# A two-block transformer on one core: attention of block 1 regrouped into units of two score tiles, and layer 1's modulation moved beside the feed-forward

## The chip, the core and the metric

One core of a Trainium2 chip runs the whole program. The engines are TensorE (PE; its weight loads are PEld), VectorE (DVE), ScalarE (ACT), GpSimd (POOL) and SyncE (SP), which here only issues transfers. They run their own instruction queues, each in order, and meet through semaphores. The metric is the device time of one execution in microseconds (us); smaller is better.

## What is computed

Two blocks of two layers each, in float32, batch 1, 512 latent tokens, 1024 features. Block 1 (layers 0 and 1) also carries 256 context tokens; its layer 1 no longer updates them.

```python
m_lat = split(silu(c) @ w_ada[li] + b_ada[li], 6)       # and m_ctx: the modulation, 6 x 1024 numbers a layer
h = rms_norm(x, g_mix) * (1 + m_lat[1]) + m_lat[0]
p = h @ w_in[li]                                        # 9 groups of 256 columns
y = concat([fourier_mix(p[:G]),
            diff_attention(p[G:4G]),                    # 4 heads, two softmaxes each, 32 wide:
                                                        #   (a0 - lam * a1) @ v, then rms_norm over 64 (the sub-norm)
            na_attention(p[4G:7G]),                     # 4 heads, 64 wide, one softmax, window bias for latent keys
            chunk_gmlp(p[7G:])])
x = x + m_lat[2] * (y @ w_out)
x = x + m_lat[5] * conv_ffn(rms_norm(x, g_ffn) * (1 + m_lat[4]) + m_lat[3])
```

Latent queries see 768 keys (512 latent and 256 context), context queries the 256 context keys. Context queries exist only in layer 0. The modulation depends on `c` and `c_ctx` alone; layer 1's is needed first by layer 1's first norm. Block 2 is another pair of layers and is not touched.

## The kernel before, in words

**Stages.** Every engine has one program (lines 2560 to 2660), the same stages in the same order: start, then for each layer of block 1 norm, projection, attention, output projection and feed-forward. There is no planner; the order on each engine is that in which the Python emits it.

**Attention of block 1** (`att_units`, line 648). The unit of work is one head for one query tile of 128: 48 units in layer 0 (2 head pairs x 6 query tiles x differential and neighbourhood x 2 heads), 32 in layer 1. `pipeline` (line 279) emits the units: in iteration u it first advances the older ones in flight, oldest first, then starts unit u, then one piece of work "beside". Each unit has four segments:

- *TensorE* (`tensor_attend`, 702): scores, with full 128-row queries that POOL has masked to the head's rows (`QM`, made at 978), against 128-row keys (721); a differential unit makes two score tiles one after the other, a neighbourhood unit one. Two iterations later up to six transposes (733), one later the value products (742) into 64 rows of bank 6.
- *VectorE* (`vector_attend`, 795): bias (838, neighbourhood and latent only), maximum (808), negated scale (810), reciprocal of the sum (815); for differential units also -lambda/sum (828), scaling of the first tile (829) and the combination with the second (831). Later the copy of 512 transposed columns (852).
- *ScalarE* (`scalar_attend`, 899): exponentials with sum (914, 922, 925), scaling for neighbourhood units (928), copy of the other 256 transposed columns (935), copy of the result into `Y` (939).
- *POOL* (`gpsimd_attend`, 966): the masked queries.

The relative-position table `TB` is loaded when the projection has read `HL` (690) and VectorE adds the window to it (800), ahead of everything else in its attention.

**Work beside** (`beside_items`, 663): statistics of the gated MLP's norm ("stat": POOL squares at 991, VectorE sums at 859, ScalarE logarithm and exponential at 945 and 947, VectorE product at 866), gated MLP, Fourier mixing, and in layer 0 the modulation: 8 pairs for layer 0 itself and 12 pairs for layer 1. A modulation pair is two 1 MB weight loads, 32 matmul records on four 32-column tiles (360), a copy by ScalarE (368), eight small records that sum and turn (374), and one VectorE instruction (381). All share bank 7, one after the other. Layer 0 gets one item an iteration, layer 1 one every third.

**After the units**: the sub-norm of `Y` columns 2 and 3 (ScalarE square 959, TensorE 790 and 792, ScalarE logarithm and exponential 962 and 964 with an activation table load each, VectorE 896).

**Output projection** (`tensor_out`, 1132; splits at 1144 to 1185). Weights are split into a high and a low part (ScalarE 1074, VectorE 1081 or POOL 1088), three views ahead; ScalarE makes three such casts before its first cast of `Y` (1153). The split of every `Y` column waits for all of attention (`y_made`, 1117). SP loads the weights as jobs of two views into three ring slots (`sync_feed`, 1041); a slot is free when both views of its former job are split.

**Feed-forward of layer 0** (`tensor_ffn` 1345, `scalar_ffn` 1375, `vector_ffn` 1405): 22 "up" steps of two views each, eight records of 768 columns times three parts a view, with four groups of eight "down" views among them. `beside` there is advanced once a step and used only in layer 1 and 2 for rotary tables.

## Time and profile before

| | |
|---|---|
| median of 3 runs | 4641.05 us (4635.44 to 4645.61) |
| the profiled execution | 4640.21 us, its span 4638.4 us |
| TensorE busy | 4199.6 us, 91% of the span |
| VectorE, ScalarE, POOL busy | 1810.7, 1468.8, 1106.0 us |
| granted TensorE clock, mean | 0.946 |

How to read it: times in the trace count from the span's start. A busy TensorE is modelled from pipelined matmuls, so the start-to-start distance of two blocks is the better measure of a rate. A float32 matmul stands as two records, a transpose as one. PEclk is the granted TensorE clock as a share of 2.4 GHz. "x8" merges eight instructions into one row. What stands in brackets is the engine's idle time before the row and what ended it.

### The profile page before, as it was taken

To read this page: it belongs to the slowest core of one execution; us is meant where nothing else is said; L and a number is where in the kernel's file an instruction comes from. 1 tells how busy PE (TensorE), PEld (TensorE's weight loads), DVE (VectorE), ACT (ScalarE), POOL (GpSimd) and SP (SyncE) were. 2 spreads that over 40 slices of the span, in tenths; PEclk is the share of its full clock that TensorE was granted. 3 is DMA by queue.
4 is the path that set the end of the run, shared out by engine and by line. 5 is a ranking of instruction groups with operands and counts; after the bars stand their busy time and mean duration, and the time that the engine had idled before them with its cause. 6 is when DMAs were issued, how large, how long until landed. Compare 5 with 4: busy or idle time off the path is not lost.

```text
span 4638.4 us, 57661 instructions
## 1 busy us (share of the span) xinstructions
PE 4199.6 (91%) x24256; PEld 3065.1 (66%) x24256; DVE 1810.7 (39%) x3078; ACT 1468.8 (32%) x2290; POOL 1106.0 (24%) x713
## 2 busy tenths in 40 slices
PE   7979889999897979999888889899998887898998
PEld 4756568888665558874445567688744455676886
DVE  1146433333214633433855421234338544213333
ACT  3245423222334433330242222333312322233332
POOL 1000132222200033331010134433210110354332
PEclk9989889999998989999998889999999988999999
DMA  4014511111101012212100022222211000222221
GB/s 187 19 61 160 222 46 55 66 64 60 66 28 47 19 63 95 96 64 73 59 19 15 25 73 95 76 91 96 89 38 59 24 10 25 74 96 71 100 96 59
DMA packets 56592, 322.35 MB, mean 69 GB/s; under 512 B 5648, under 2 KB 5776, under 8 KB 27920
## 3 DMA queue, kind: packets, MB, share of 16 engines
q1 hardware_dynamic: 56336, 318.67, 19.4%
q8 instruction: 193, 3.16, 0.3%
q14 instruction: 63, 0.52, 0.0%
HBM read 316.55 MB, written 2.10 MB: 69 GB/s over the span
## 4 chain that ended last, share of the span: by engine, by line
PE 78%; DVE 11%; ACT 5%; issue 3%; POOL 2%; DMA 1%; SPq 0%; POOLq 0%; DVEq 0%; ACTq 0%
PE ps L1101 47%; PE ps L1563 5%; PE ps L547 4%; PE ps L538 3%; PE ps L2005 3%; PE ps L721 2%; PE ps L742 2%; PE ps L322 1%; PE ps L360 1%; PE ps L733 1%; PE ps L2085 1%; POOL WL L1088 1%; DVE ar L1819 1%; DVE small L1815 1%; PE ps L781 1%
## 5 line engine op out<-in xcount | busy, mean ns | idle before, releaser
L1088 POOL TENSOR_TENSOR WL<-ring,WH 128x1024 fp32r<-128x1024 f32 (+4 forms) x262 | 572.3, 2185 | 1153.8 <-ACT WH L1074 1132.0
L1074 ACT ACTIVATE WH<-ring 128x1024 fp32r<-128x1024 f32 (+4 forms) x408 | 397.7, 977 | 1293.0 <-PE ps L1101 1287.2
L1101 PE MATMUL ps<-FH,WH 128*128 128x512 f32 x1760 | 602.6, 375 | 42.7 <-POOL FL L1271 37.7
L1101 PE MATMUL ps<-FH,WL 128*128 128x512 f32 x1760 | 599.5, 374 | 0.0
L1101 PE MATMUL ps<-FL,WH 128*128 128x512 f32 x1760 | 595.1, 371 | 0.0
L1436 DVE SCALAR_TENSOR_TENSOR ftmp<-ps,vec,ftmp 128x511 f32<-128x511 f32 (+2 forms) x440 | 302.0, 695 | 347.6 <-ACT ftmp L1393 193.1
L1081 DVE TENSOR_TENSOR WL<-ring,WH 128x1024 fp32r<-128x1024 f32 (+4 forms) x146 | 164.1, 1129 | 639.0 <-ACT WH L1074 638.9
L1101 PEld LDWEIGHTS ps<-FH,WH 128*128 128x128 f32 x1760 | 309.0, 190 | 114.2 <-issue 45.2
L1101 PEld LDWEIGHTS ps<-FL,WH 128*128 128x128 f32 x1760 | 310.4, 190 | 60.2
L1101 PEld LDWEIGHTS ps<-FH,WL 128*128 128x128 f32 x1760 | 308.6, 190 | 59.9
L1101 PE MATMUL ps<-AH,WH 128*128 128x512 f32 x880 | 308.2, 383 | 9.8 <-DVE AL L1441 9.8
L1101 PE MATMUL ps<-AH,WL 128*128 128x512 f32 x880 | 299.9, 374 | 0.0
L1101 PE MATMUL ps<-AL,WH 128*128 128x512 f32 x880 | 297.9, 371 | 0.0
L1563 PE MATMUL ps<-HL,ring 128*128 128x512 f32 x448 | 199.7, 602 | 4.3 <-DVE HL L1555 3.6
L721 PE MATMUL ps<-ar,HC 128*128 128x256 f32 (+1 forms) x432 | 156.7, 498 | 33.6 <-ACT ar L914 31.2
L1101 PEld LDWEIGHTS ps<-AH,WH 128*128 128x128 f32 x880 | 155.0, 190 | 44.4 <-DVE AL L1441 11.4
L1459 POOL TENSOR_TENSOR ftmp<-ftmp 128x512 f32<-128x512 f32 (+1 forms) x88 | 126.1, 1433 | 219.6 <-DVE ftmp L1436 219.2
L1101 PEld LDWEIGHTS ps<-AL,WH 128*128 128x128 f32 x880 | 155.0, 190 | 34.2 <-issue 4.3
L1101 PE MATMUL ps<-GH,WH 128*128 128x512 f32 x384 | 153.2, 399 | 23.7 <-POOL GL L2528 23.7
L1101 PEld LDWEIGHTS ps<-AH,WL 128*128 128x128 f32 x880 | 154.2, 189 | 29.5
L1563 PEld LDWEIGHTS ps<-HL,ring 128*128 128x128 f32 x448 | 86.2, 194 | 112.6 <-issue 108.1
L978 POOL TENSOR_TENSOR HC<-ar,cst 128x512 f32<-128x512 f32 (+1 forms) x40 | 32.9, 844 | 527.1 <-PE ps L721 334.0
(404 smaller groups left out, 7261.9 us busy)
## 6 DMA issues: line engine op xcount, KB each, us to landing
ring<-in_wup SPq DMA_DIRECT2D x88, 1024.0 KB, 4.8
ring<-in_wada SPq DMA_DIRECT2D x30, 1024.0 KB, 6.4
ring<-in_wgate SPq DMA_DIRECT2D x24, 1024.0 KB, 4.8
ring<-in_wdown SPq DMA_DIRECT2D x24, 896.0 KB, 4.7
ringb<-in_wada SPq DMA_DIRECT2D x18, 1024.0 KB, 6.4
ring<-in_wout SPq DMA_DIRECT2D x16, 1024.0 KB, 4.8
ring<-in_wdown SPq DMA_DIRECT2D x12, 1024.0 KB, 5.0
ring<-in_wbr SPq DMA_DIRECT2D x24, 512.0 KB, 3.3
```

The lines of the kernel that those rows point to most:

```text
L538: mm = e.matmul(pr[:, b * 512:b * 512 + 256], h[:, k, :], wt[:, k * 256:k * 256 + 256], start=k == 0, stop=k == 7)
L547: mm = e.matmul(pr[:, c:c + n], wt[:, k * 256 + j * 128:k * 256 + j * 128 + 128], h[:, k, :], start=k == 0, stop=k == 7)
L721: mm = e.matmul(pr[:, n:n + b - a], q, PF[:, base + jt, a:b], start=True, stop=True)
L742: mm = e.matmul(bank(6)[p0:p0 + 64, 0:128], PT[:, b, col + h * 64:col + h * 64 + 64], tmp1(3)[:, x * 128:x * 128 + 128], start=x == 0, sto ...
L1074: e.activation(wh, view, ACT.Copy).then_inc(*whi_a.up(L, n))
L1081: e.tensor_tensor(wl, view, wh.bitcast(F32), SUB).then_inc(*wlo_v.up(L, n))
L1088: e.tensor_tensor(wl, view, wh.bitcast(F32), SUB).then_inc(*wlo_g.up(L, n))
L1101: mm = e.matmul(out[:, c:c + h.shape[1]], ww[:, k, :], h, start=at == 0 and p == 0, stop=at == K - 1 and p == 2)
L1436: e.scalar_tensor_tensor(out=dst, in0=src, scalar=conv_cols(L, ch, a), in1=dst, op0=MUL, op1=ADD).then_inc(*(ffn_v.up(L, "tap", x, j, c) i ...
L1459: e.tensor_tensor(zg, zg, zv, MUL).then_inc(*ffn_g.up(L, x))
L1563: mm = e.matmul(out, wt[:, k * step + off:k * step + off + 128], HL[:, k, :], start=k == 0, stop=k == 7)
L2005: mm = e.matmul(out, wt[:, k * step + off:k * step + off + 128], HL[:, k, :], start=k == 0, stop=k == 7)
```

## The change

1. `att_units` now lists units of two score tiles: a differential unit is one head (its two softmaxes), a neighbourhood unit is a head pair. 36 units in layer 0, 24 in layer 1, in the order: two differential units of query tile g, then the neighbourhood unit of g-1.
2. Scores are made without masked queries: the two tiles use the head's own 32 (differential) or 64 (neighbourhood) rows of queries and keys, issued in turn into two different bank pairs. `QM` and POOL's masking go. A unit's scores wait until the unit before has been read.
3. Transposes go to banks 4 (copied by VectorE) and 5 (copied by ScalarE), three blocks each; the weights of two heads lie in two buffers in the space that `QM` had, and the value products of two heads are issued in turn into the two halves of bank 6. ScalarE copies 128 rows at once.
4. The scaling of a differential unit's first tile moves from VectorE (829) to ScalarE. The two reciprocals become one of two columns.
5. The window is added to `TB` by POOL, as its first instruction in attention.
6. The sub-norm runs as work beside, column by column and (layer 0) in a 512- and a 256-part, in a new buffer `adab`. The order in which `Y` is split and used becomes 0, 1, 6, 7, 2, 4, 3, 5.
7. Layer 1's 12 modulation pairs move to layer 0's feed-forward: one part or sum before each "up" view. Their weights go to `adab`, one part at a time; the transfers are issued by SP in between those of the weight jobs, and the first of them right behind job 0.
8. Beside items are placed by a plan: layer 0 one an iteration, layer 1 one every second.

The core of the diff (the engines' programs in attention are shown where the order of instructions matters):

```diff
+        E = [[tmp1(0), tmp1(1)], [tmp1(2), tmp1(3)]]
+        WT = [hcf[:, 768 * i:768 * i + 768] for i in range(2)]
...
+            groups = [(jt, *q) for jt in range(2) for q in qts]
+            for g in range(len(groups) + 1):
+                if g < len(groups):
+                    out += [(groups[g][0], "diff", hh, *groups[g][1:]) for hh in range(2)]
+                if g:
+                    out.append((groups[g - 1][0], "na", None, *groups[g - 1][1:]))
...
+            for x, it in enumerate(beside_items(l)):
+                plan[x if l == 0 else 2 * x].append(it)
+            for j in (2, 3):
+                for p in range(2 if l == 0 else 1):
+                    plan[last_diff(l, j) + 4 + p].append(("sq", j, p))
+                    plan[last_diff(l, j) + 5 + p].insert(0, ("root", j, p))
...
@@ tensor_attend, unit
+                if u:
+                    w.wait_ge(*scores_taken(l, u - 1, 0), *scores_taken(l, u - 1, 1))
+                for c, d_ in kcols:
+                    for a in range(2):
+                        r = slice(64 * hh + 32 * a, 64 * hh + 32 * a + 32) if sort == "diff" else slice(64 * a, 64 * a + 64)
+                        mm = e.matmul(two(a)[:, n:n + d_ - c], PF[r, BASE[kq] + jt, qc:qc + 128], PF[r, BASE[kk] + jt, c:d_],
+                                      start=True, stop=True)
...
+                for x, b in enumerate(vb):
+                    for a in range(2):
+                        mm = e.matmul(bank(6)[64 * a:64 * a + 64, 0:128], PT[:, b, c:c + 64], WT[a][:, x * 128:x * 128 + 128], start=x == 0,
+                                      stop=x == len(vb) - 1)
...
@@ vector_attend, unit: segment 1 bias, maximum, shift of both tiles; then
+                w.wait_ge(soft_a.at(l, u, "exp", 0), soft_a.at(l, u, "exp", 1))
+                e.reciprocal(inv, total).then_inc(*soft_v.up(l, u, "inv"))
+                if sort == "diff":
+                    e.tensor_scalar(top[:, 0:1], inv[:, 1:2], nlam, None, MUL).then_inc(*soft_v.up(l, u, "nlam"))
+                    w.wait_ge(soft_v.at(l, u, "nlam"), soft_a.at(l, u, "w0"))
+                    e.scalar_tensor_tensor(out=E[u % 2][0][:, 0:n], in0=E[u % 2][1][:, 0:n], scalar=top[:, 0:1], in1=E[u % 2][0][:, 0:n],
+                                           op0=MUL, op1=ADD).then_inc(*soft_v.up(l, u, "w"))
...
@@ scalar_attend, unit: segment 1 exponentials of both tiles; then
+                w.wait_ge(soft_v.at(l, u, "inv"))
+                for a in range(1 if sort == "diff" else 2):
+                    e.activation(x, x, ACT.Copy, scale=inv[:, a:a + 1]).then_inc(...)
...
@@ gpsimd_attend
+            w.wait_ge((in_rpb, 16 * (l + 1)))
+            e.tensor_tensor(TB2, TB2, C("win")..., ADD).then_inc(*tb_g.up(l))
...
+        def mods1_after(j):
+            out = [] if j else [0]
+            for i in range(1, 24):
+                t = MODS1.index(("part", i - 1))
+                if (view_of(0, "up", t // 2, t % 2) + 7) // 2 == j:
+                    out.append(i)
+            return out
@@ sync_feed, after the load of job j
+                for i in mods1_after(j) if L == 0 else ():
+                    w.wait_ge(*([mod_mm.at(1, i - 1, "part")] if i else [sub_v.at(0, 2, 1), sub_v.at(0, 3, 1)]))
+                    for r in range(2):
+                        e.dma_start(adab[:, r, :], d["wada"][1, i][:, 1024 * r:1024 * r + 1024]).then_inc(ada_in[r], 16)
...
+        MODS1 = [(x, i + b) for i in range(0, 24, 2) for x, b in (("part", 0), ("part", 1), ("sum", 0))]
...
@@ tensor_ffn
+                        next(beside, None)
@@ scalar_ffn, vector_ffn
-                next(beside, None)
                 for j in range(2):
+                    if L == 0 or j == 0:
+                        next(beside, None)
```

## Rows read from the trace of the kernel before

**Rows 1.** Busy time by stretch: us, each engine with its instructions, granted clock, DMA share, GB/s

```profile
400.00:530.00 130.00, 127.84 (x1123) 89.94 (x1123) 81.45 (x215) 67.32 (x163) 8.06 (x10) 1.00 0.64 243
530.00:562.00 32.00, 19.69 (x136) 11.26 (x135) 5.06 (x9) 15.10 (x17) 0.00 (x0) 0.62 0.54 220
1465.00:1625.00 160.00, 144.98 (x766) 99.23 (x766) 108.71 (x220) 77.55 (x173) 8.57 (x10) 0.96 0.06 20
720.00:760.00 40.00, 40.00 (x232) 35.02 (x231) 16.00 (x24) 11.65 (x13) 10.92 (x5) 1.00 0.20 67
2650.00:2670.00 20.00, 11.28 (x196) 7.05 (x187) 6.63 (x14) 4.51 (x5) 0.00 (x0) 0.60 0.00 1
```

**Rows 2.** Timeline of layer 1's attention, TensorE: start, us, instructions

```profile
1530.92 0.87 PE L733 MATMUL ps<-cst,ar 128*128 128x128 f32 x6
...
1531.63 2.75 PE L721 MATMUL ps<-ar,HC 128*128 128x512 f32 x8
```

**Rows 3.** Timeline of layer 1's attention, VectorE and ScalarE

```profile
1449.80 0.68 DVE L838 SCALAR_TENSOR_TENSOR ar<-ps,HL 128x512 f32<-128x512 f32 x1
...
1452.75 0.16 DVE L815 RECIPROCAL small<-small 128x1 f32<-128x1 f32 x1 [1.10 <-ACT ar L922]
...
1452.95 0.94 ACT L928 ACTIVATE ar<-ar,small 128x768 f32<-128x768 f32 x1 [0.23 <-DVE small L815]
...
1453.79 0.25 ACT L939 ACTIVATE ar<-ps 64x128 f32<-64x128 f32 x1
...
1453.94 0.36 ACT L935 ACTIVATE ar<-ps 128x256 f32<-128x256 f32 x1
...
1465.28 0.95 DVE L808 TENSOR_REDUCE small<-ps 128x1 f32<-128x768 f32 x1
...
1468.52 0.16 DVE L815 RECIPROCAL small<-small 128x1 f32<-128x1 f32 x1 [0.89 <-ACT ar L914]
...
1469.50 1.02 DVE L831 SCALAR_TENSOR_TENSOR ar<-ar,small 128x768 f32<-128x768 f32 x1
```

**Rows 4.** Timeline where layer 1's attention starts

```profile
1422.84 2.32 POOL L991 TENSOR_TENSOR ar<-ar 128x256 f32<-128x256 f32 x4
...
1428.83 4.16 DVE L800 TENSOR_TENSOR HL<-HL,cst 128x3840 f32<-128x3840 f32 x1 [44.23 <-DMA HL<-in_rpb]
...
1438.06 0.41 DVE L859 TENSOR_REDUCE small<-ar 128x4 f32<-128x256 f32 x1
...
1443.69 0.43 DVE L866 TENSOR_TENSOR ar<-ar,small 128x256 f32<-128x256 f32 x1 [2.70 <-ACT small L947]
```

**Rows 5.** Timeline of layer 0's attention, TensorE, with a modulation pair

```profile
459.51 1.93 PE L360 MATMUL ps<-ring,silp 128*32 128x256 f32 x32
...
461.37 1.52 PE L742 MATMUL ps<-ar 128*64 128x128 f32 x12
...
464.83 0.95 PE L374 MATMUL ps<-cst,modp 128*128 128x2 f32 x8
...
465.71 1.52 PE L742 MATMUL ps<-ar 128*64 128x128 f32 x12
```

**Rows 6.** Timeline of block 2's recurrence, TensorE: two row tiles

```profile
2411.06 0.69 PE L2011 MATMUL ps<-cst,ring 64*128 64x512 f32 x1
...
2411.06 0.69 PE L2013 MATMUL ps<-cst,ring 64*128 64x512 f32 x1
```

**Rows 7.** Timeline, ScalarE, where the two attention stages end

```profile
558.67 2.94 ACT L1074 ACTIVATE WH<-ring 128x1024 fp32r<-128x1024 f32 x3
...
1631.15 1.28 ACT L962 ACT_TABLE_LOAD   x1
...
1634.44 0.63 ACT L964 ACTIVATE ar<-ar 128x512 f32<-128x512 f32 x1
```

**Rows 8.** DMA issues of layer 0's feed-forward: count, KB each, median us to landing

```profile
ring<-in_wup SPq DMA_DIRECT2D x18, 1024.0 KB, 4.8
```

More of the change, by code:

```diff
@@ L668, in beside_items @@
             if l == 0:
-                out += [(x, li, i) for li, a in ((0, 8), (1, 0)) for i in range(a, 24, 2) for x in ("parts", "sum")]
+                out += [(x, 0, i) for i in range(8, 24, 2) for x in ("parts", "sum")]
             return out
@@ L795, in vector_attend @@
         def vector_attend(e, w, l):
[L796 removed]
+            units = att_units(l)
             nlam = tiny[:, 85:86]
[L798 to L804 removed]
@@ L856, in item @@
+            def item(it):
                 if it[0] == "stat":
@@ L929, in unit @@
-                yield 1
-                yield 1
-                if kind == "lat":
-                    w.wait_ge(turn_mm.at(l, u))
-                    if u:
-                        w.wait_ge(pv_mm.at(l, u - 1))
-                    e.activation(tmp1(3)[:, 512:n], two(2)[:, 512:n], ACT.Copy).then_inc(*wt_a.up(l, u))
+                top, shift, total, inv = soft_stat(u)
+                biased = sort == "na" and kind == "lat"
+                if u >= 2:
+                    w.wait_ge(*(turn_mm.at(l, u - 2, c, k) for c, _, k in turns_of(l, u - 2)))
@@ new lines, in unit @@
+                for a in range(2) if biased else ():
+                    w.wait_ge(qk_mm.at(l, u, a))
+                    e.activation(E[u % 2][a][:, 512:n], two(a)[:, 512:n], ACT.Copy, scale=0.125).then_inc(*soft_a.up(l, u, "ctx", a))
+                for a in range(2):
+                    x = E[u % 2][a][:, 0:n]
+                    w.wait_ge(soft_v.at(l, u, "shift", a))
+                    if biased:
+                        w.wait_ge(soft_a.at(l, u, "ctx", a))
+                    e.activation(x, x if biased else two(a)[:, 0:n], ACT.Exp, bias=shift[:, a:a + 1],
+                                 scale=1.0 if biased else 32 ** -0.5 if sort == "diff" else 0.125,
+                                 accum_out=total[:, a:a + 1]).then_inc(*soft_a.up(l, u, "exp", a))
@@ L991, in item @@
                         e.tensor_tensor(LB[:, 256 * (t % 4):256 * (t % 4) + 256], v, v, MUL).then_inc(*loc_g.up(l, t))
-            pipeline([unit(u, *x) for u, x in enumerate(units)], beside(l, item))
+            pipeline([unit() for _ in att_units(l)], beside(l, item))
         def chunks_of(n):
@@ L1132, in tensor_out @@
         def tensor_out(e, w, l):
-            last, turns = len(att_units(l)) - 1, soft_turns(l)
+            last = len(att_units(l)) - 1
             segs = segs_of(l)
```

361 lines of the change are left out of this document (178 added, 183 removed).

## The prediction

> **What bounds the kernel now.** I read the busy time by stretch first, because the average over the span hides the stages. The change touches four stretches: the attention of layer 0 (about 257 to 562 us), the attention of layer 1 (1421 to 1643), and, since work moves there, the feed-forward of layer 0 (678 to 1190); the rest of the span is untouched. In attention TensorE is busy 127.8 of 130 us in layer 0 and 145.0 of 160 in layer 1, VectorE 81 and 109, ScalarE 67 and 78 [rows 1]. So TensorE sets the pace there. Layer 1 has eight groups of four units in those 160 us: 20.0 us a group. Only the end of layer 0's stretch is slack: after the last unit, from about 530, modulation pairs run alone, with the clock granted at 0.62 [rows 1]. In the feed-forward TensorE is busy 40.00 of 40 us [rows 1]: whatever is put on it there costs its full price.
>
> The timeline of one unit says what TensorE pays: two score tiles 2.75 us for eight records (2.57 us of steady streaming), six transposes 0.87 (0.65 start to start), six value products 1.52 [rows 2, 5]. A group of two differential and two neighbourhood units is 2 x 5.1 + 2 x 3.9 = 18.0 us of TensorE out of 20.
>
> **What the edits do to TensorE.** Scores: each unit now issues two tiles on different row tiles into different banks. Block 2 has such a pair: two 64-row, 512-column matmuls start at the same 2411.06 us [rows 6]. Halving takes 3 x 1.28 = 3.8 us off a group. Values: pairs in column tiles; the modulation's four 32-column tiles run 32 records of 256 columns in 1.86 us [rows 5], about 58 ns each, where one alone would be some 213, so a pair should fit in the time of one: another 3 us. TensorE then needs 18.0 - 3.8 - 3 = some 11 us a group. It no longer sets the pace, and the question is what comes next.
>
> The Trainium skill (TensorEngine Tiling, Key Properties) says that changing the tiling mode, not just the tile, drains TensorE, and the new units change it three times each. That rule speaks against the row and column tiles; it gives no figure. In the trace the four-tile block is followed by two-tile work 1.86 us after its start and shows no gap beyond its own 1.93 us [rows 5]. I put 0.1 us on each insertion in the feed-forward and nothing on it in attention, where TensorE has slack; at 0.5 us a change attention would still not move, and the feed-forward would take 15 more.
>
> **What is late next: a chain through ScalarE and VectorE.** VectorE's queue in iteration u is: copies of unit u-2, combine of u-1, maxima of u. ScalarE's: value copy of u-3, weights copies of u-2, scaling of u-1, exponentials of u. The scaling waits for the exponentials of u-1, the combine waits for the scaling, the maxima stand behind the combine, the exponentials behind the maxima: one serial loop. Steps from rows:
> - maxima of both tiles to both exponentials done: 1468.52 - 1465.28 = 3.2 us [rows 3];
> - scaling 0.94, combine 1.02 (0.94 to the next start) [rows 3];
> - ScalarE's copies ahead of the scaling: value copy 0.15 start to start, weights copy of 384 columns about 0.38 (256 columns take 0.36) [rows 3];
> - a biased tile, bias to sum: 1452.75 - 1449.80 = 2.95, and the second tile adds 0.68 + 0.95 + 0.15 = 1.8.
>
> Second differential unit: 0.15 + 2 x 0.38 + 0.94 + 0.94 + 3.2 = 6.0. Neighbourhood unit behind it: 0.15 + 0.38 + 0.94 + 0.03 + 0.94 + 2.95 + 1.8 = 7.2. First differential unit behind that has no combine ahead: 0.38 + 2 x 0.83 + 2 x 1.05 = 4.2 on ScalarE. Group: **17.4 us** against 20.0. The three removals on VectorE (the first tile's scaling, a third of each weights copy, one reciprocal) are in these numbers; the scaling has only moved to ScalarE, where it is on the loop.
>
> **Starts.** The bias add leaves VectorE (4.16 us, and the wait for its table before it) for POOL, so the first maxima come some 8 us sooner. But POOL's squares now queue behind it, and VectorE waits for them in its first beside item. Before, that item began at 1438.06. Now: table at 1428.8, the add on POOL (3840 columns; 256 take 0.58, so at most 8.7 and, with the fixed part off, I take 8), squares 0.6: 1437.5. The start gains 0.5 us a layer, nothing more; were POOL as quick as VectorE it would be 4. The statistics keep their 6 us an item, 1438.06 to 1444.1 [rows 4].
>
> **Layer 1.** Statistics and three units to 1466; then 8 x 7.2 + 6 x 6.0 + 6 x 4.2 = 119 us; beside copies 2; the first sub-norm, now in the loop on ScalarE (3.9 us with its two table loads, 1631.15 to 1635.07, plus a square) 4.4 [rows 7]; TensorE queueing behind Fourier items and some cold stretches 12, an estimate. That is 1603.5 for the last exponential; two more scalings, copies, transposes and value products of the last unit 6.5; the second sub-norm 3.9: 1614, against 1635.1: **-21 us**.
>
> **Layer 0.** Statistics (three items) and three units to 303, as before. Then one more unit, 5.5; eight latent groups less the first units, 8 x 7.2 + 6 x 4.2 + 6 x 6.0 = 119; four context groups at 256 columns, 8.2 each, 33; TensorE queueing 12; ScalarE's beside items (4 Fourier copies, 8 modulation copies, 0.5 each) and VectorE's overhang 7; the first column's sub-norm in two parts 8.3: 488 for the last exponential, 491 for the last value copy, and, after two parts with two table loads each (7.7), 499 for the last sub-norm. Before, this point was 558.7, where the weight casts start [rows 7]: -60. Of these, some 50 are the twelve modulation pairs that leave, the last of which ran alone.
> Then a **new wait**: the first modulation load for layer 1 is queued on SP behind weight job 0 and waits for the last sub-norm, since it lands in the buffer that the sub-norm uses. Jobs 1 and 2 stand behind it. ScalarE's third weight cast needs job 1 and stands ahead of the casts of Y. A 1 MB load lands in 4.8 us [rows 8]; behind another MB I take 7.6 (about 2.8 us a MB, an estimate: 243 GB/s at a DMA share of 0.64 [rows 1] makes 380 GB/s in full), so job 1 arrives some 8.5 us after the sub-norm, where the cast would have been due 2 us after: +7. Net of layer 0's attention: **-53 us**.
>
> **Feed-forward of layer 0.** Twelve pairs, each 1.86 for the parts and 0.88 for the sum [rows 5]: 32.9 us, all on the path. 36 insertions at 0.1 us: 3.6. Loads: one buffer, so the load of part i waits for part i-1. In six pairs out of twelve the odd part comes one view (8.3 us, 48 of 232 records in 40) later while a ring job is ahead of it in the queue: landing near 10.7 us against a need at 9.25, 1.5 x 6 = 9. What ScalarE and VectorE do for a pair lies beside: they are busy 11.7 and 16.0 of 40 us there [rows 1]. **+45 us**; bounds 33 (no gap, no stall) and 60 (each odd part 2 us late).
>
> **Sum.** -53 - 21 + 45 = -29 us. The profiled execution took 4640.2, its span 4638.4, and the median of the runs is 4641.05, 0.8 above; so 4612 on the median's scale. A measurement of this kernel tells a change from none at about 0.2%, 9.3 us.
>
> **Rivals.**
 Cold, a group needs some 21 us of TensorE and it is the bound again: 3.7 x 8 = 30, less the 9 already taken, +21: 4632, the same as before within the measurement. Against it: layer 0 has modulation beside, and a cold engine is a busier one. Chance 0.17. The Trainium skill (TensorE: Matmul & The Clock Gate, Loop structure matters more than you think) says that matmuls stay warm or not by the loop nest, and that waits between them make them run cold. By that rule this rival would come true; the row of 0.60 agrees.
> - *The modulation starves the feed-forward* (slower). Place: the odd part's wait for its load. A load that waits behind two others, at 2.8 us for each MB more, is 10 us under way. If each of the twelve odd parts waits 5 us, that is 60, not 9, and the time 4662; it turns the sign at 3.3 us a part. For it: a single buffer. Against it: DMA is only 20% busy there [rows 1]. Together with a loop 10% longer than I count: 0.14.
> - *The loop is shorter*: copies overlap, table loads fall into ScalarE's waits, job 1 is in time. 10% of 290 us of loop and the 7: about 4578. Chance 0.19.
> - *Row tiles don't overlap* in fp32: TensorE 15 of 17.4 us and the scores at 2.8 us, about when the combine ends: 4620. It lies within the forecast.
>
> **How the numbers follow.** Forecast (4595 to 4628) 0.50, shorter 0.19, clock 0.17, slower 0.14. Faster takes the first two and a part of the third, 0.74; same 0.13; slower 0.13. Range 4578 to 4650: from the short loop to just past no change.
>
> **What would show it.** Groups in layer 1 near 17.4 us with VectorE or ScalarE ending most waits; TensorE about 65% busy there; first maxima near 1424 but first statistics still near 1437 less the shift; a gap of some 7 us on ScalarE ahead of its third weight cast of layer 0; the feed-forward of layer 0 longer by 36 to 60. Wrong if attention keeps TensorE above 85%, if a group is over 19 us, or if the feed-forward grows by more than 60.

## The result, and the profile after

The changed kernel takes 4668.5 us (median of 7 runs, 4657.6 to 4673.9), the kernel before 4638.8 in the same session: a ratio of 1.0058, with a 95% interval of 1.0045 to 1.0072. By the ratio it is **slower by some 27 us** (the medians are 29.7 us apart), where 29 us less were forecast. The profiled execution took 4657.6 us with a span of 4655.8.

Three marks divide the span for everything below: TensorE's first sum of squares in layer 0's output projection (P0, which stands a tile and a half behind that projection's start, so that waits at its start are in it), its first scores of layer 1 (S1), and its first sum of squares in layer 1's output projection (P1). In the changed kernel they are these lines of TensorE's timeline (start, us, instructions, the idle time before them):

```profile
567.99 1.24 PE L324 MATMUL ps<-ytmp,cst 128*128 128x512 f32 x3
...
1457.12 1.56 PE L773 MATMUL ps<-ar 32*128 32x512 f32 x8 [0.78 <-ACT ar L608]
...
1680.59 1.02 PE L324 MATMUL ps<-ytmp,cst 128*128 128x512 f32 x2
```

| stage | before | after | difference | forecast |
|---|---|---|---|---|
| to P0 (all up to the start of layer 0's output projection; the changed part is its attention) | 586.7 | 568.0 | -18.7 | -53 |
| P0 to S1 (output projection and feed-forward of layer 0, norm and projection of layer 1) | 835.7 | 889.1 | +53.4 | +45 |
| S1 to P1 (layer 1's attention, start of its output projection) | 233.0 | 223.5 | -9.5 | -21 |
| sum | 1655.3 | 1680.6 | +25.3 | -29 |

Behind P1 nothing is changed; in the profiled executions of all kernels here that rest takes between 2974 and 2989 us, so spans of single executions are not compared below, but the stages. Each mark comes from one execution: P0 to S1, all but the same in this kernel and in eight of the runs below (e1, e5, e6, e9, e13, e14, e16, e17), lies between 887.5 and 892.2 us there, so a difference of 2 or 3 us in it says nothing.

Busy time by stretch of the kernel after (columns as in [rows 1]: us, PE, PEld, DVE, ACT, POOL with their instructions, granted clock, DMA share, GB/s):

```profile
303.00:400.00 97.00, 83.03 (x523) 52.02 (x520) 63.95 (x145) 55.84 (x123) 0.00 (x0) 0.89 0.13 44
400.00:505.00 105.00, 79.21 (x657) 51.69 (x658) 53.27 (x126) 62.78 (x130) 0.00 (x0) 0.80 0.32 121
505.00:560.00 55.00, 29.79 (x173) 19.58 (x174) 22.14 (x38) 23.13 (x45) 13.01 (x6) 0.69 0.20 77
720.00:760.00 40.00, 39.16 (x264) 31.63 (x252) 12.62 (x20) 13.11 (x16) 11.62 (x6) 1.00 0.34 118
1484.00:1650.00 166.00, 120.70 (x786) 74.98 (x787) 100.07 (x201) 102.06 (x197) 0.00 (x0) 0.84 0.04 14
```

TensorE is no longer full in attention: 162 of 202 us in layer 0 and 121 of 166 in layer 1, where [rows 1] had 128 of 130 and 145 of 160. No engine is; each waits for another, and the granted clock in layer 1 has gone from 0.96 to 0.84. In the feed-forward it is 39.2 of 40 us busy, as before.

The sub-norm's place in layer 1, TensorE's and ScalarE's timeline:

```profile
1569.40 0.61 ACT L985 ACTIVATE adab<-ar 128x512 f32<-128x512 f32 x1
1570.16 2.05 PE L817 MATMUL ps<-adab,cst 128*128 128x512 f32 x2 [6.26 <-ACT adab L985]
1572.00 1.38 PE L784 MATMUL ps<-cst,ar 128*128 128x128 f32 x6
1573.31 1.56 PE L773 MATMUL ps<-ar 32*128 32x512 f32 x8
...
1578.14 1.28 ACT L989 ACT_TABLE_LOAD   x1
1579.44 0.69 ACT L989 ACTIVATE adab<-ps,cst 128x512 f32<-128x512 f32 x1
1580.14 1.28 ACT L991 ACT_TABLE_LOAD   x1
1580.18 5.27 PE L842 MATMUL ps<-ring,ar 128*128 128x512 f32 x8 [5.31 <-ACT adab L989]
...
1585.38 1.53 PE L798 MATMUL ps<-HC,ar 128*64 128x128 f32 x24
```

Here is what the forecast did not have. The sum of squares (L817) stands in TensorE's queue ahead of the next unit's transposes and scores, and the square that it waits for stands on ScalarE behind both exponentials: TensorE stands still for 6.3 us. One iteration later the Fourier product (L842) wants PSUM bank 7, which the logarithm reads; that stands behind two more exponentials and a table load: another 5.3 us, and then the product runs cold, 5.3 us where it takes 3.7 at full clock. Values, transposes and scores are behind it.

The end of layer 0's attention, ScalarE and SP's queue:

```profile
533.12 1.99 ACT L1114 ACTIVATE WH<-ring 128x1024 fp32r<-128x1024 f32 x2
533.82 0.80 SPq L1089 DMA_DIRECT2D adab<-in_wada  x2
534.67 2.37 SPq L261 DMA_DIRECT2D ring<-in_wout  x3
542.21 1.06 ACT L1114 ACTIVATE WH<-ring 128x1024 fp32r<-128x1024 f32 x1 [7.11 <-DMA ring<-in_wout]
```

The third cast waits 7.1 us for a job that is queued behind the first modulation load: as forecast, 7.

The start of layer 1's attention, VectorE and POOL:

```profile
1458.68 0.96 DVE L871 TENSOR_REDUCE small<-ps 128x1 f32<-128x768 f32 x1 [38.93 <-PE ps L773]
...
1464.01 8.27 POOL L1004 TENSOR_TENSOR HL<-HL,cst 128x3840 f32<-128x3840 f32 x1 [93.33 <-DMA HL<-in_rpb]
1472.23 2.33 POOL L1018 TENSOR_TENSOR ar<-ar 128x256 f32<-128x256 f32 x4
1472.88 0.42 DVE L896 TENSOR_REDUCE small<-ar 128x4 f32<-128x256 f32 x1 [12.00 <-POOL ar L1018]
```

The order is as forecast: the first maxima come 1.6 us after the first scores. The first statistics come 15.8 us after the scores, against 15.7 in the kernel before, so the 0.5 us that the forecast took for a start is not there.

The groups of TensorE's instructions between 680 and 1280 us that are the modulation (parts, sums; busy us, mean ns, idle time before them; eleven of the twelve pairs, the first begins at 640.6 us, ahead of that window), and the places where its load is on the chain of work that ended last (start, us):

```profile
L1405 PE MATMUL ps<-adab,silp 128*32 128x256 f32 x352 | 25.2, 392 | 8.6 <-DMA adab<-in_wada 8.6
...
L376 PE MATMUL ps<-cst,modp 128*128 128x2 f32 x88 | 10.4, 241 | 0.0
```

```profile
692.04 7.71 DMA adab<-in_wada
752.98 6.46 DMA adab<-in_wada
...
1089.19 6.12 DMA adab<-in_wada
```

There are six such places, one for every second pair, as counted beforehand. TensorE waits for these loads 8.6 us in all, 1.9 us at most at a time; the forecast had 9.

### The profile page after: what moved, and what is told of

It is laid out like the page before. It is cut to its first block, busy times and chain, and to the rows that moved or that the text cites. A ratio compares the mean times of both kernels' runs of the same rounds, so it can differ in the third digit from the quotient of the medians.

```text
span 4655.8 us, 57676 instructions
## 1 busy us (share of the span) xinstructions
PE 4136.1 (89%) x24256; PEld 2999.5 (64%) x24256; DVE 1760.1 (38%) x2974; ACT 1496.2 (32%) x2304; POOL 1089.6 (23%) x675
## 4 chain that ended last, share of the span: by engine, by line
PE 70%; DVE 11%; issue 8%; ACT 6%; POOL 3%; DMA 2%; SPq 0%; POOLq 0%; DVEq 0%; ACTq 0%
PE ps L1141 46%; PE ps L1637 5%; PE ps L2079 3%; PE ps L549 2%; PE ps L324 1%; DVE small L871 1%; POOL WL L1128 1%; DMA adab<-in_wada 1%; PE ps L798 1%; PE ps L540 1%; PE ps L773 1%; PE ps L2159 1%; PE ps L784 1%; DVE ar L1893 1%; DVE small L1889 1%
## 5 line engine op out<-in xcount | busy, mean ns | idle before, releaser
L1141 PE MATMUL ps<-GH,WL 128*128 128x512 f32 x384 | 152.0, 396 | 0.0
L1141 PE MATMUL ps<-GL,WH 128*128 128x512 f32 x384 | 150.8, 393 | 0.0
```

The costliest lines, as they stand in the source:

```text
L1141: mm = e.matmul(out[:, c:c + h.shape[1]], ww[:, k, :], h, start=at == 0 and p == 0, stop=at == K - 1 and p == 2)
```

## The experiments

Two theories at first. **Queue**: the sub-norm beside the units, priced in the forecast at its time on ScalarE, holds TensorE's queue and bank 7, and costs two to three times that. **Clock**: attention falls short since TensorE, now with pauses, runs at the lower level. All ratios are against the kernel before, with their 95% intervals. The marks of the profiled executions:

| run | to P0 | P0 to S1 | S1 to P1 | ratio |
|---|---|---|---|---|
| kernel before | 586.7 | 835.7 | 233.0 | 1 |
| changed kernel | 568.0 | 889.1 | 223.5 | 1.0058 |
| e1_subnorm_end | 549.6 | 887.5 | 217.0 | 1.0002 |
| e5_sum_one_later | 553.8 | 892.2 | 218.1 | 1.0032 |
| e4_warm | 587.1 | 883.7 | 240.2 | 1.0127 |
| e9_squares_first | 565.0 | 887.7 | 216.9 | 1.0053 |
| e2_no_mods | 560.8 | 844.4 | 224.2 | 0.9933 |
| e3_one_load | 566.0 | 878.7 | 223.4 | 1.0028 |
| e6_first_load_later | 561.1 | 890.6 | 226.1 | 1.0050 |
| e7_mods_in_attention | 615.7 | 844.3 | 223.8 | 1.0056 |
| e10_copy_later | 620.0 | 841.9 | 217.0 | 1.0045 |
| e8_best | 608.7 | 840.9 | 206.3 | 0.9991 |
| e11_before_wider | 583.3 | 835.8 | 235.3 | 1.0002 |
| e13_best_mods_ffn | 537.5 | 891.6 | 204.6 | 0.9934 |
| e14_copy_same | 530.4 | 889.9 | 206.3 | 0.9916 |
| e16_roots_shared | 526.5 | 889.8 | 203.0 | 0.9907 |
| e17_both | 525.9 | 889.3 | 203.9 | 0.9908 |

### e1_subnorm_end: the sub-norm undone

```
 beside_plan:
-            for j in (2, 3):
-                for p in range(2 if l == 0 else 1):
-                    plan[last_diff(l, j) + 4 + p].append(("sq", j, p))
-                    plan[last_diff(l, j) + 5 + p].insert(0, ("root", j, p))
 tensor_attend, after the pipeline (scalar_attend and vector_attend likewise, as before the change):
+            for j in (2, 3):
+                w.wait_ge(sub_a.at(l, j, 1 - l, "sq"), *scores_taken(l, last, 0), *scores_taken(l, last, 1))
+                mm = e.matmul(two(j - 2)[:, 0:512], C("b64"), tmp1(j)[:, 0:512], start=True, stop=True)
```

> The changed kernel with one part undone: the sub-norm of both columns after the last unit, in the two score tiles, as before the change. Changed kernel: ratio 1.0058 to the kernel before, about 4668 us. Theory 'the sub-norm beside holds up TensorE's queue': in layer 1 it costs about 14 us where it stands (the iteration of 32.4 us for a group that takes 18.4), in layer 0 about 15; at the end a column costs 4 to 5 us more in each layer. So shorter by 18 to 22 us: about 4648, ratio 1.0015. Rival 'it costs no more than its time on ScalarE' (4.4 and 8.3 us, which are paid at the end too): no change within 4 us, 4668. Rival 'the clock explains the short gain of attention': no change either, with the granted clock still 0.83 to 0.85 in the loops.

Measured: 4638.5 us, 1.0002 [0.9994, 1.0011], 26 us less than the changed kernel. Expected were 18 to 22. Its marks have 18.4 us of it in layer 0 (2.0 of them ahead of the first scores, where nothing was edited) and 6.5 in layer 1. The cost stands: the sub-norm beside was dearer than the sub-norm at the end, by 25 us, in a change that put it there to be hidden. The group of units that took 32.4 us in layer 1 takes 22.7; in layer 0 one that took 35.1 takes 15.4.

The loops by themselves, from the first scores of a layer to its last, are 257.8 us (layer 0) and 179.3 (layer 1) in the changed kernel, 240.3 and 169.3 in e1. So the first column's sub-norm costs the loops 17.5 and 10.0 us; the forecast had 8.3 and 4.4. What follows the last scores is 1.2 and 3.5 us longer in e1.

The groups of e1 in layer 1 say something besides, with no sub-norm among them: from one neighbourhood unit's scores to the next they take 18.3, 22.7, 17.7, 22.7, 17.7 and 18.8 us. The two of 22.7 are those in which a Fourier product stands beside the group's first differential unit. The second of them in e1's timeline (TensorE and VectorE):

```profile
1549.67 5.56 PE L838 MATMUL ps<-ring,ar 128*128 128x512 f32 x8
...
1555.16 1.53 PE L794 MATMUL ps<-HC,ar 128*64 128x128 f32 x24
...
1557.21 0.56 DVE L892 COPY HC<-ps 128x384 f32<-128x384 f32 x1 [5.26 <-PE ps L780]
```

Values and transposes of older units are behind the product in TensorE's queue; VectorE's copy of the transposed weights waits 5.3 us for them, and the combination and the next maxima stand behind that copy. The product runs cold here (5.6 us, 5.0 in the other group, 3.7 at full clock), which is at most 1.9 of the 5.0 us. So TensorE's queue is a part of the loop even where an item waits for nothing.

### e5_sum_one_later: the same place on ScalarE, another on TensorE

```
-                    plan[last_diff(l, j) + 5 + p].insert(0, ("root", j, p))
+                    plan[last_diff(l, j) + 5 + p].insert(0, ("root", j, p))
+                    plan[last_diff(l, j) + 5 + p].insert(0, ("sqm", j, p))
+                    plan[last_diff(l, j) + 6 + p].insert(0, ("prod", j, p))
 and the other items, which use bank 7 too, are placed around the iterations of "sqm"
```

> The changed kernel with the sub-norm still beside the units, but its TensorE sum one iteration after the square, no other user of the eighth PSUM bank in that iteration, and the product on VectorE one more iteration later. ScalarE's own work (square, two table loads, two activations) is the same and in the same place. Theory 'queue': most of the excess goes, 10 us in layer 1 and 8 in layer 0 (the second column's tail stays): about 4650. Rival 'the table loads on ScalarE are the price': within 3 us of the changed kernel, 4668.

Measured: 4651.3, 1.0032 [1.0019, 1.0045]: 12 us less than the changed kernel by the ratios, 17 by the medians; its marks say 14.2 in layer 0 and 5.4 in layer 1, of which its feed-forward, 3 us longer in that execution, hides a part. So between half and four fifths of e1's gain is there, although ScalarE does the same work at the same place. The sum no longer waits (TensorE's timeline of this run, with ScalarE's square ahead of it):

```profile
1558.94 0.61 ACT L994 ACTIVATE adab<-ar 128x512 f32<-128x512 f32 x1
...
1559.87 2.08 PE L826 MATMUL ps<-adab,cst 128*128 128x512 f32 x2
...
1569.84 3.70 PE L851 MATMUL ps<-ring,ar 128*128 128x512 f32 x8
```

The loops are 246.9 and 175.4 us, 6.6 and 6.1 more than in e1: 12.7 us, which is what the forecast had for this work (8.3 and 4.4). What lies above the forecast, another 14.8 us in the changed kernel, is therefore no time of ScalarE's but comes from where the sum stands. The edit changes two things together, the place of the sum in TensorE's queue and the neighbours in bank 7; what each is worth was not separated.

### e4_warm: more work for TensorE while it waits

```
+                for _ in range(4):
+                    e.matmul(bank(bk)[:, 0:256], C("ident"), C("cos1")[:, 0:256], start=True, stop=True)
                 for a, blocks, bk in turns_of(l, u):
                     w.wait_ge(soft_v.at(l, u, "w") if sort == "diff" else soft_a.at(l, u, "w", a))
```

> The changed kernel with four extra 256-column products of a constant in every unit of both attentions, issued while TensorE waits for the weights to transpose and written over by the transposes; results unchanged. They take 0.85 us at full clock. Rival 'clock': the granted clock rises from 0.84 to over 0.95 in the loops, Fourier blocks fall from 5.3 to 3.7 us and modulation parts from 3.6 to 1.9, and the time falls by 15 to 25 us, to about 4648. Theory 'queue, and the serial loop through VectorE and ScalarE': those blocks mostly lie beside, the gain is under 8 us, and where the extra work delays a transpose it is lost again: 4660 to 4672.

Measured: 4695.6, 1.0127 [1.0114, 1.0140], 32 us **more** than the changed kernel. Neither theory said so. The granted clock did rise (0.92 against 0.88 in 1500 to 1650), and the Fourier product came down to 3.7 us, but four extra products took 1.9 us and not 0.85 (an fp32 product is two records; by the 3072 columns in 2.57 us of [rows 2] eight records of 256 columns are 1.7 us), and the transposes behind them start late:

```profile
1560.60 3.70 PE L846 MATMUL ps<-ringb,ar 128*128 128x512 f32 x8
1564.14 1.89 PE L783 MATMUL ps<-cst 128*128 128x256 f32 x8
1565.87 0.82 PE L788 MATMUL ps<-cst,ar 128*128 128x128 f32 x6
1566.62 1.56 PE L773 MATMUL ps<-ar 32*128 32x512 f32 x8
```

I had sized the extra work wrongly, so the run does not give the price of the clock. It shows something else: 60 units with 1.9 us more each, 114 us, cost 32, although TensorE had pauses of 27% on average. Its pauses are not where its work is. A higher clock without that work was not tried.

### e9_squares_first: the order on POOL

```
+            for t in range(4):
+                squares(t)
             TB2 = TB.rearrange("p h y x -> p (h y) x")
             w.wait_ge((in_rpb, 16 * (l + 1)))
             e.tensor_tensor(TB2, TB2, C("win")...
```

> The changed kernel with POOL's squares of the first four row blocks issued before its 8.3 us add of the window to the bias table, instead of behind it. Theory 'the add on POOL is what keeps the first statistics late': the first statistics sum on VectorE comes 8 us sooner in each layer, the table is ready 2.5 us later than now, still before the third unit: shorter by 10 to 16 us, about 4655. Rival 'the third unit then waits for the table': shorter by less than 5 us.

Measured: 4659.9, ratio 1.0053 [1.0041, 1.0065]; its interval overlaps the changed kernel's. The gain is 2 us by the ratios and 9 by the medians; the marks show 3.0 us in layer 0 and 6.6 in layer 1. All are less than the 10 to 16 expected. The statistics do start at once, but their product on VectorE stands still while POOL adds (VectorE's and POOL's timeline of this run):

```profile
1459.49 8.26 POOL L1013 TENSOR_TENSOR HL<-HL,cst 128x3840 f32<-128x3840 f32 x1 [5.70 <-DMA HL<-in_rpb]
...
1460.62 7.75 DVE L903 TENSOR_TENSOR ar<-ar,small 128x256 f32<-128x256 f32 x2 [3.13 <-ACT small L981]
```

Two products that take 0.43 us each elsewhere end at 1468.4, 0.6 us after POOL is done. The Trainium skill (SBUF — State Buffer, Who interferes with whom) says that a VectorE instruction which holds the SBUF ports that it shares with GpSimd, and one of GpSimd, exclude each other for their whole length; its section on the two sides of SBUF counts two SBUF inputs on VectorE among the cases. The trace agrees: 7.75 us for two products of two SBUF inputs. ScalarE, TensorE's transposes and the next maxima wait behind these products, not for the table, so the rival's reason did not come true, and whether its size did the ratios and the medians leave open.

### e2_no_mods and e3_one_load: what the feed-forward's 53.4 us are

e2 leaves out layer 1's modulation and uses layer 0's in its place; e3 leaves out the weights of all parts but the first.

```
e2: -        MODS1 = [(x, i + b) for i in range(0, 24, 2) for x, b in (("part", 0), ("part", 1), ("sum", 0))]
    +        MODS1 = []
    -                for i in mods1_after(j) if L == 0 else ():
    +                for i in ():
e3: -                for i in mods1_after(j) if L == 0 else ():
    +                for i in [0] if L == 0 and j == 0 else ():
    -                    w.wait_ge((ada_in[r], 16 * (i + 1)))
    +                    w.wait_ge((ada_in[r], 16))
```

> The changed kernel without layer 1's modulation: neither its loads nor its products nor its sums are there, and layer 1 uses layer 0's modulation instead. Changed kernel: ratio 1.0058, about 4668. Theory 'the whole growth of layer 0's feed-forward, 54 us by the two traces, is the twelve modulation pairs, and the 7 us wait of the third weight cast is their first load': shorter by 58 to 62 us, about 4608, ratio 0.993. Rival 'part of the growth is something else in the feed-forward': shorter by less than 50. Beside the kernel before, which has these pairs under its attention, it would say what the regrouped attention, sub-norm as it is, gives when TensorE has no layer-1 modulation anywhere.

> The changed kernel with all 24 modulation parts of layer 1 taken from one load, so that no part waits for its weights and 23 MB are not loaded; the products are all there. It leaves out the weights of parts 1 to 23 (layer 1's modulation is computed from the first part's). Theory 'the price in the feed-forward is TensorE's own time, 36 us and more, the waits for loads are about 9 to 14': shorter by 9 to 14, about 4656. Rival 'starved feed-forward': shorter by over 25, below 4643.

Measured: e2 4608.7, 0.9933 [0.9917, 0.9950]; e3 4652.5, 1.0028 [1.0017, 1.0040]. Both times are as expected. The marks split the 53.4, each term to within the 2 or 3 us of one execution: reloads 889.1 - 878.7 = **10.4** us (forecast 9), products and insertions 878.7 - 844.4 = **34.3** (forecast 36.5), together 44.7 against 45 in the forecast. But e2, with no modulation there at all, still takes 844.4 where the kernel before takes 835.7: **8.7 us** that are no part of the modulation (e7, e10 and e8, also without it there, take 844.3, 841.9 and 840.9). This is e2's rival, and for its size the marks decide, not the time. It comes in very small pieces. Busy time by stretch of the kernel before, and of e2:

```profile
800.00:1000.00 200.00, 200.00 (x1148) 175.15 (x1147) 62.47 (x96) 47.66 (x53) 52.19 (x26) 1.00 0.21 69
```

```profile
800.00:1000.00 200.00, 200.00 (x1134) 174.27 (x1133) 62.74 (x96) 48.99 (x54) 50.38 (x24) 1.00 0.19 64
```

Both are full and at the full clock, and yet 1148 records go through in one and 1134 in the other: 1.2% slower, with nothing to wait for.

### e11_before_wider: is it where the tiles lie?

```
 modp = sb("modp", [P, 2, 512])
+adab = sb("adab", [P, 2, 1024])
```

> The kernel before with nothing but the 8 KB tile added that the change allocates; no instruction uses it, but all tiles behind it lie 8 KB further in every partition. In the two changed kernels that have no modulation in layer 0's feed-forward, TensorE's pairs of 512 and 256 columns follow each other every 0.353 us there, in the kernel before every 0.349, and the stage from the first output projection to layer 1's first scores takes 866 us against 857. Theory 'the placement of the tiles does that': slower by 8.7 us, ratio 1.0019. Rival 'it comes with the program, not with the tiles': ratio 1.0000.

Measured: 4642.2, 1.0002 [0.9994, 1.0011], and 835.8 us from P0 to S1. A shift of the tiles by 8 KB is not it. e8 below, without that tile, has 1134 records again. The rate goes with the program, in a way that no run here explains.

### e6_first_load_later

```
-            out = [] if j else [0]
+            out = [0] if j == 2 else []
```

> The changed kernel with the first modulation load behind weight job 2 instead of job 0 on SP, so that jobs 1 and 2 do not wait for the last sub-norm. Theory 'that wait costs 7 us': 4661, and the gap of 7.1 us on ScalarE before its third weight cast is gone. Rival 'the output projection would wait for the casts of the values anyway': under 2 us.

Measured: 4664.6, 1.0050 [1.0032, 1.0068]: by the ratios not to be told from the changed kernel. In the profile the gap is gone and P0 comes 6.9 us sooner; the two stages behind it were 4 us longer together in that execution. The place is confirmed by the mark, the gain of the whole only within its interval.

### e7, e10: the modulation back beside the attention

```
e7:  -                plan[x if l == 0 else 2 * x].append(it)
     +                plan[(x if x < 19 else 19 + (x - 18) // 2) if l == 0 else 2 * x].append(it)
e10: sub-norm at the end as in e1, and on ScalarE
     -                    scalar_mod(e, w, it[1], it[2], bank(7))
     +                    pending.append(it[1:])
     and flush() of what is pending ahead of the next unit's exponentials
```

> The changed kernel with layer 1's modulation back beside layer 0's attention, as before the change, but with the sum of one pair and the parts of the next in the same iteration, so that the 20 pairs of both layers fit in 21 iterations. Theory 'TensorE has room there and none in the feed-forward': the feed-forward falls by 54 us, the 7 us wait goes, layer 0's attention grows by some 2 us a pair, 24 us: shorter by 37, about 4631, ratio 0.998. Rival 'each pair holds up the queue or its 2 MB come too late': attention grows by 45 or more, 4652, ratio 1.003.

> The kernel with the sub-norm at the end (ratio 1.0002, 4639 us) with layer 1's modulation back beside layer 0's attention, one pair in one iteration, and ScalarE's copy of a pair's parts one iteration later, ahead of the exponentials instead of behind them, in which ScalarE had waited 48 us for the parts of 20 pairs. Theory 'the pairs cost what ScalarE waits for them, TensorE has the room': the feed-forward gives 45 us back, the wait of the third cast 7, layer 0's attention grows by 15: 4602, ratio 0.992. Rival 'the parts hold up TensorE's queue all the same, since they wait for VectorE's sum (28 us over 19 pairs)': attention grows by 35 or more: 4622, ratio 0.9965.

Measured: e7 4664.3, 1.0056 [1.0037, 1.0075]; e10 4662.3, 1.0045 [1.0033, 1.0057]. Both rivals, and worse. The feed-forward gives back 45, and layer 0's attention takes it all: P0 comes 47.7 us later in e7 than in the changed kernel, and 70.3 later in e10 than in e1, although no 7 us wait is left. For each of twelve pairs, with the gap of 7 us that went, that makes 4.6 us in e7 and 6.5 in e10; a pair cost 3.7 in the feed-forward. One iteration of e10, in order of time:

```profile
447.00 1.05 PE L376 MATMUL ps<-cst,modp 128*128 128x2 f32 x8 [0.40 <-ACT modp L370]
...
449.61 0.16 DVE L383 TENSOR_TENSOR small<-ps,vec 128x8 f32<-128x8 f32 x1
...
449.82 3.64 PE L362 MATMUL ps<-ring,silp 128*32 128x256 f32 x32 [1.77 <-DVE small L383]
453.39 2.31 PE L794 MATMUL ps<-HC,ar 128*64 128x128 f32 x24
...
455.75 0.28 ACT L987 ACTIVATE ar<-ps 128x128 f32<-128x128 f32 x1 [5.03 <-PE ps L794]
```

TensorE waits for VectorE's sum, then the parts run cold (3.64 us against 1.93 in [rows 5]), then come the values, and ScalarE waits 5.0 us for them with the scaling behind. In the kernel before, TensorE was the bound, busy 127.8 of 130 us at a granted clock of 1.00, and a pair took 2.7 us of its time there [rows 5]. In the regrouped attention a pair is neither hidden nor cheap. Which of the two places is better is less clear: e7 has the ratio of the changed kernel (1.0056 and 1.0058). e10 is 20 us slower than e1, but it also has the later copy, which e14 below finds to cost 7.1 us for eight pairs; by that rate its twenty pairs would have 18 us of it (an estimate).

### e8, e13, e14, e16, e17: towards a kernel that beats both

```
e13 (on e1): first modulation load without its wait for the sub-norm; scalar_mod one iteration later, as e10;
     squares(t) for t in range(4) ahead of all on POOL; in vector_attend, first statistics item, before the products:
+                    if 0 in it[1]:
+                        w.wait_ge((in_rpb, 16 * (l + 1)))
+                        e.tensor_tensor(TB2, TB2, C("win")..., ADD).then_inc(*soft_v.up(l, "tb"))
     sub-norm at the end: Ln, Ln, Exp, Exp in place of Ln, Exp, Ln, Exp
e8:  e13 with the modulation beside the attention (as e10), and no adab
e14: e13 with scalar_mod in the same iteration
e16: e13 with a statistics item's Ln, Ln, Exp, Exp
e17: both
```

> As the run above, and besides: POOL's first four squares ahead of everything, the window added to the bias table by VectorE while ScalarE takes the first roots (4.2 us on VectorE, in a wait of 6), the two columns' logarithms together and their exponentials together at the end (two table loads less a layer), and the 8 KB tile of the modulation's loads not allocated. Theory: 10 us sooner at each of the two starts, 2.6 at each end, and 8.7 in the feed-forward if the placement of the tiles is what makes its products 1.4% slower: 4602 - 20 - 5 - 9 = 4568, ratio 0.985. Rival 'the starts are given back, since the third unit waits for its table and the loop for the weights' transposes': 4590.

> The kernel with the sub-norm at the end (4639 us) and layer 1's modulation left in the feed-forward, its first load not waiting for the sub-norm; besides, as in the second run of these four: squares first, the table by VectorE, the copy of the parts one iteration later, tables loaded once for both columns. Theory: 7 for the wait of the third cast, 20 for the two starts, 5 for the ends: 4607, ratio 0.993; the difference to the second run, 39 us, is what the place of the modulation and the tile cost. Rival 'starts given back': 4625.

> The fastest kernel so far (sub-norm at the end, modulation in the feed-forward, squares first, table by VectorE; ratio 0.9934, 4609 us) with ScalarE's copy of layer 0's modulation parts back behind the exponentials of the same iteration. Theory 'that copy waits for cold parts and holds up the loop': longer by 8 us (8 pairs, 1 us each): 4617, ratio 0.995. Rival 'it changes nothing, since with the later copy the sum waits in TensorE's queue instead': 4609.

> The fastest kernel so far (4609 us) with the two logarithms of a statistics item together and then the two exponentials, so that an item has two table loads (1.28 us each) instead of four. Theory 'ScalarE's table loads lie on the serial loop': five items, 2.6 us each less, 13 us, but in the first item of each layer VectorE's table add of 4.2 us now ends last, so 10: 4599, ratio 0.991. Rival 'ScalarE's time beside is hidden': under 3 us.

> The run with ratio 0.9934 with both edits: the copy of the parts in the same iteration (0.9916 alone) and one pair of table loads a statistics item (0.9907 alone). Theory 'different places, they add up': 0.9934 - 0.0018 - 0.0027 = 0.989, about 4590. Rival 'they share a wait, or each was a matter of the placement of the program': 0.9907, 4598.

Measured: e8 4632.5, 0.9991 [0.9981, 1.0002], far from 4568: it carries e10's price, the later copy of twenty pairs included. e13 4609.2, 0.9934 [0.9922, 0.9946], as expected. Layer 1's attention is down to 204.6 us from 217.0 in e1, 12.4 for the start and the tables. VectorE's add lies in ScalarE's root time, out of POOL's way.

e14: 4602.5, 0.9916 [0.9903, 0.9930], where slower or the same was expected. Its interval overlaps e13's a little, but the marks agree that it is faster. With the later copy TensorE's sums wait 11.9 us for it in 303 to 505 us, with the copy in place 2.8; P0 comes 7.1 sooner. The later copy, of e10 too, was a mistake of mine: it took a wait off ScalarE and put it on TensorE's queue. TensorE's groups of e13 and of e14 in that stretch:

```profile
L376 PE MATMUL ps<-cst,modp 128*128 128x2 f32 x64 | 10.2, 282 | 11.9 <-ACT modp L370 11.9
```

```profile
L376 PE MATMUL ps<-cst,modp 128*128 128x2 f32 x64 | 9.5, 271 | 2.8 <-ACT modp L370 2.8
```

e16: 4598.1, 0.9907 [0.9893, 0.9920], as expected: P0 comes 11.0 us sooner than in e13, layer 1's attention is 1.6 shorter. So the table loads of the statistics lie on the loop, more in layer 0 (three items) than in layer 1 (two; in the first the exponentials are done at 1424.9 and the products begin at 1427.2, when VectorE's table add ends). e17: 4595.6, 0.9908 [0.9894, 0.9921]: its rival; the two do not add up (P0 at 525.9 against 526.5). The fastest kernels here are e16 and e17 (e14 is within their intervals), **0.9% faster than the kernel before**, 1.5% than the changed one.

## Why the prediction was wrong

Forecast 4612, measured 4668.5, outside the range of 4578 to 4650 and of the other sign.

- **The step that failed: "one serial loop" of ScalarE and VectorE alone, with what stands beside it priced at its own time and TensorE's queue put at 12 us a layer ("TensorE has slack").** The runs show TensorE's queue inside that loop: whatever holds it delays the transposes, and through VectorE's copies the next maxima. By the marks the forecast missed by 54 us: 34 in layer 0's attention, 12 in layer 1's, 8 in the feed-forward.
- **Its clearest term: "the first sub-norm, now in the loop on ScalarE 4.4" and, in layer 0, "the first column's sub-norm in two parts 8.3".** 12.7 us, measured 27.5 (17.5 and 10.0). The item was followed neither through TensorE's queue nor through bank 7. It makes a group 32.4 us long that takes 22.7 in e1, and in layer 0 35.1 instead of 15.4. e5, without touching ScalarE's work, brings it back to 12.7. With this term alone right the forecast would have been 4627, still 12 us below the kernel before: out of the loops it takes the slowdown away (e1 is at 1.0002), but it is not all of the miss.
- **Its larger term: layer 0's loop without the sub-norm, some 20 us.** The forecast has the last exponential at 488, 479.7 without its 8.3; in e1 it is done at 499.6. The forecast gave TensorE's queue 12 and the other items 7 there. Groups of a latent neighbourhood unit and two latent differential units, forecast at 17.4, take 20.5 to 21.4 in e1's layer 0, with an item in every iteration, and 17.7 in its layer 1 where no Fourier product stands beside the first differential unit. Four of the eight parts run cold in e1's layer 0, 1.7 us more each, and two Fourier products of 256 columns, 1 us more each, so the clock can be 9 of these 20 (an estimate). Which item costs how much was not separated: that TensorE's queue is the cause here is read from timelines, and no run shows it by itself.
- **Layer 1's loop.** "17.4 us a group" was 18.3, 21.6, 19.2, 17.7 and 19.0 where no sub-norm is. The last exponential is done 187.7 us after S1 where the forecast has 181.1, and 5.6 of these 6.6 us are the sub-norm; so its 12 for TensorE's queue was about right here. From there to the last value copy it takes 11.6 us and not 6.5: the last unit was priced too low.
- **The modulation in the feed-forward, +45**: 44.7 by e2 and e3, both terms within 2.2 us. The rival "the modulation starves the feed-forward" found its place, six reloads on the chain, but not its size: 8.6 us of waits in all, near the 9 that were counted, not 60.
- **8.7 us that no step had**: TensorE's products of layer 0 run 1.2% slower at full clock in every kernel with the new attention and no modulation in the feed-forward. Not a shift of the tiles (e11). Open.
- **Row tiles and column tiles**: eight records of two score tiles take 1.56 us against 2.75 [rows 2], 24 value records 1.53 against 1.52 for 12. They do what the forecast says. "TensorE has slack in attention" was true on average (80% busy in layer 0, 73% in layer 1) and false for what it was used for: that extra work in the queue costs nothing.
- **The 7 us at the third cast** were right, the starts nearly so (nothing in place of 0.5 us); that a later load can take the 7 us away is shown by its gap in e6, not by e6's time.
- **The rival of the clock**: granted 0.84 in place of 0.96, and cold parts and Fourier products. Half of the rival came true: the clock fell. But its group of 21 us, with TensorE as the bound, did not: TensorE is 73% busy in layer 1. And e1 and e5 changed the time while the clock stayed at 0.82 to 0.86 in the loops. Its own price stays open, since e4 was badly sized; where items run cold it is 1.3 to 1.9 us each.
- "Wrong if a group is over 19 us" came true, and so did nothing else of that list.

## What to carry to other kernels

An item put "beside" a loop has a price on every engine whose queue it stands in: for each of its instructions ask what it waits for in its own iteration, and what stands behind it. A sum placed in the iteration of its square, or a bank handed over in the iteration of its last reader, costs the loop the whole wait; one iteration later that wait is gone (e5). But a later place is no rule by itself: ScalarE's later copy of the modulation parts took a wait off ScalarE and put a longer one on TensorE's queue (e13 against e14). Once the bounding engine is relieved, its loop becomes a chain through all engines, and work that was hidden under the bound can then be on the chain, a part of it at the lower clock. Measure the old place again before relying on it, in either direction.

## What the hardware showed that was not expected

- VectorE products with two SBUF inputs stood still behind a POOL add: 7.75 us for two that take 0.43 each.
- At a granted clock of 1.00, without a wait, the same stream of products ran at 1148 records in 200 us in two kernels (before, e11) and at 1134 in four others (e2, e7, e8, e10), one traced execution of each.
- A product placed beside the loop held up VectorE although TensorE was idle a quarter of the time: 5.3 us behind a Fourier product of 5.6 us (e1).
